# Norms of a two-block network in two parts of the tokens, 384-token matmul ranges, and weight splits two tiles ahead

## The reference

```python
x = x + mix @ w_out                                  # out-projection
h2 = rmsnorm(x, norm2_w)                             # y = x * rsqrt(mean(x*x) + eps) * w, over a token's features
x = x + jnp.square(jax.nn.relu(h2 @ w_ff1)) @ w_ff2  # MLP, 4096 wide
```

## Time and profile before

| | us |
|---|---|
| median of 3 runs | 2395.6 |
| all runs | 2392.7, 2411.45, 2395.6 |
| profiled execution, its own time | 2409.31 |
| its span in the profile | 2407.5 |
| PE busy in the span | 2305.8 |
| mean granted PE clock, of full speed | 0.983 |

### The profile page before, as it was taken

One profiled execution on the slowest core, in us unless ns is written; L12 is line 12 of the kernel. 1 busy time (PEld: TensorE's weight loads), 2 busy tenths in 40 slices (PEclk: granted clock), 3 DMA queues, 4 the chain that ended last, 5 costly groups with the idle time before them and its releaser, 6 DMA issues.

```text
span 2407.5 us, 29863 instructions
## 1 busy us (share of the span) xinstructions
PE 2305.8 (96%) x11514; PEld 1828.8 (76%) x11514; DVE 1409.9 (59%) x2253; ACT 901.5 (37%) x1536; POOL 514.6 (21%) x385
## 2 busy tenths in 40 slices
PE   7989799999999998989999999999999999999998
PEld 5655577888877875668888888888776568888887
DVE  5475648888667456773565565543635774534435
ACT  4254533232333224882422222122422684423232
POOL 2332214232312210001312121111120001322221
PEclk9999899999999999999999999999999999999999
DMA  4211016555411221011243343321122112222321
GB/s 162 88 62 54 27 35 235 193 192 203 167 66 57 93 96 34 22 36 36 84 140 123 118 136 123 123 101 59 58 96 80 32 45 70 102 89 96 109 88 53
DMA packets 76248, 227.69 MB, mean 95 GB/s; under 512 B 9151, under 2 KB 12608, under 8 KB 76108
## 3 DMA queue, kind: packets, MB, share of 16 engines
q1 hardware_dynamic: 70928, 216.69, 26.5%
q0 software_dynamic: 1856, 6.07, 0.7%
q10 hardware_dynamic: 3324, 3.02, 0.4%
HBM read 220.99 MB, written 4.76 MB: 94 GB/s over the span
## 4 chain that ended last, share of the span: by engine, by line
PE 84%; DVE 7%; ACT 4%; issue 3%; POOL 2%; ACTq 0%; DMA 0%; DVEq 0%; SPq 0%; POOLq 0%
PE psum L685 33%; PE psum L949 25%; PE psum L1256 3%; PE psum L715 3%; PE psum L654 3%; PE psum L1287 2%; PE psum L735 2%; PE psum L1210 2%; PE psum L1145 1%; PE psum L1271 1%; PE psum L603 1%; PE psum L1104 1%; PE psum L1223 1%; PE psum L1171 1%; DVE mod_scratch L1440 1%
## 5 line engine op out<-in xcount | busy, mean ns | idle before, releaser
L685 PE MATMUL psum<-mix_split,weight_split 128*128 128x512 f32 (+1 forms) x3456 | 701.3, 364 | 2.3 <-POOL weight_split L2743 1.3
L685 PEld LDWEIGHTS psum<-mix_split,weight_split 128*128 128x128 f32 x3456 | 589.8, 188 | 110.4 <-POOL weight_split L2743 1.7
L949 PE MATMUL psum<-hidden,weight_split 128*128 128x512 f32 (+1 forms) x3072 | 623.2, 364 | 0.6 <-DVE residual L1736 0.6
L949 PEld LDWEIGHTS psum<-hidden,weight_split 128*128 128x128 f32 x3072 | 523.5, 188 | 96.9 <-DVE weight_split L1362 1.0
L2193 ACT CAST weight_split<-weight_ring 128x1024 fp32r<-128x1024 f32 x269 | 277.1, 1041 | 298.4 <-PE psum L949 235.6
L2743 POOL TENSOR_TENSOR weight_split<-weight_ring,weight_split 128x1024 fp32r<-128x1024 f32 x89 | 233.0, 2618 | 597.1 <-ACT weight_split L2193 596.5
L1721 DVE TENSOR_TENSOR hidden<-hidden_tmp,hidden 128x512 fp32r<-128x512 f32 (+1 forms) x128 | 156.0, 1238 | 305.9 <-POOL hidden_tmp L2864 305.9
L1362 DVE TENSOR_TENSOR weight_split<-weight_ring,weight_split 128x1024 fp32r<-128x1024 f32 x180 | 233.8, 1301 | 39.8 <-ACT weight_split L2193 39.8
L2864 POOL TENSOR_TENSOR hidden_tmp<-hidden_tmp 128x512 f32<-128x512 f32 (+1 forms) x128 | 127.5, 1007 | 598.3 <-ACT hidden L2446 598.0
L2442 ACT ACTIVATE hidden_tmp<-psum 128x512 f32<-128x512 f32 (+1 forms) x128 | 69.2, 541 | 482.8 <-PE psum L685 481.8
L1738 DVE SCALAR_TENSOR_TENSOR residual<-psum,modulation,residual 128x512 f32<-128x512 f32 x192 | 120.2, 657 | 156.3 <-PE psum L949 155.9
(11 more groups left out here) (317 smaller groups left out, 2483.7 us busy)
## 6 DMA issues: line engine op xcount, KB each, us to landing
weight_ring<-in_w_mlp SPq DMA_DIRECT2D x128, 512.0 KB, 3.8
weight_ring<-in_w_ff SPq DMA_DIRECT2D x64, 512.0 KB, 4.4
mod_ring<-in_w_mod SPq DMA_DIRECT2D x48, 512.0 KB, 3.5
late_ring<-in_w_mod SPq DMA_DIRECT2D x96, 256.0 KB, 3.4
weight_ring<-in_w_in SPq DMA_DIRECT2D x45, 512.0 KB, 3.5
weight_ring<-in_w_out SPq DMA_DIRECT2D x24, 512.0 KB, 3.4
weight_ring<-in_tables SPq DMA_DIRECT2D x13, 512.0 KB, 3.5
weight_ring<-in_w_v SPq DMA_DIRECT2D x8, 512.0 KB, 3.9
```

The costliest lines, as they stand in the source:

```text
L685: m = pe.matmul(psum[:, b + r, 0:hi - lo], w[:, part_w, :], x[:, part_x, k, lo:hi], start=k == 0 and part_w + part_x == 0, stop=k == KT - ...
L949: mm = pe.matmul(psum[:, b + r, 0:hi - lo], w[:, part_w, :], G[:, part_x, f % (2 * GROUP), lo:hi], start=jj == 0 and part_w + part_x == 0, ...
```

## The change

It has four pieces.

1. **384-token ranges.** Copy 0's out-projection (tiles 0 to 3), up products (from tile 2 on) and down products (all groups but the last) take `halves_of(0) = [(0, 384), (384, 768)]` in place of 512 and 256. ACT's relu and square then cover both banks in one instruction, and DVE adds the result to `X` in three pieces (0:384, 384:512, 512:768), since the gate differs from token 512 on.
2. **Norms in two parts.** For `n2` and `l1n2` the parts are tokens 0 to 255 and 256 to 511; for `l0n2` and `l1n1` tokens 0 to 511 and the context. The last four output tiles ahead of the norm (all eight down tiles for `l1n1`) are made for the first part and then for the second, with the first part's sums and spread between the second part's tiles, and no `keep_busy`. The next product's first two tiles follow in the same two parts, with the second part's sums and spread between their input tiles.
3. **Splits two weight tiles ahead** in the in-projection (`in2_two_on`) and out-projection (`two_on`), whatever tables lie between.
4. **The first two tiles of `w_out2`** are now declared before the mid stage's tables, and split at the end of the in-projection; the split in the attention is gone.

The diff, cut to its core (ACT and POOL follow DVE's order):

```diff
+        def parts_of(norm):
+
+            cut = S if norm in ("l0n2", "l1n1") else S // 2
+            return [(norm + "a", 0, cut), (norm + "b", cut, T2 if cut == S else S)]
...
+        def up_spans(ranges, f):
+
+            return XB if len(ranges) > 1 and f < 2 else [(0, ranges[-1][1])]
...
+        def halves_of(l):
+
+            return X1 if l else [(0, T2 // 2), (T2 // 2, T2)]
...
+        def two_on(name, m):
+
+            return load_at[name(m + AHEAD)] if m + AHEAD < KT else load_at[name(m)] + AHEAD
+
+        def in2_two_on(l, i):
+
+            return load_at["w_in2", (l, IN2[i + AHEAD][0])] if i + AHEAD < 14 else load_at["w_in2", (l, IN2[i][0])] + AHEAD
...
+            def part_sums(norm, p):
+
+                tag, lo, hi = parts_of(norm)[p]
+                token_sums(tag, [sums_and_last(tag, SQ[:, 0, :], SQ[:, 1, :], lo, hi)], (tag + "_act", ("root", lo)), 0)
+
+            def part_spread(norm, p):
+
+                tag, lo, hi = parts_of(norm)[p]
+                b = on_all_partitions(tag, (hi - lo) // P, c=lo, n=1)
+                freed[b] = [(tag + "_vec", ("scaled", KT - 1, 0))]
+
             def norm(tag, nt, last, squares=None):
 
...
+            def product_in_parts(tag, tiles, x, spans, order=range(KT)):
+
+                at = [use_load(*w, split=True) for _, w in tiles]
+                for p, (lo, hi) in enumerate(spans):
+                    for (i, _), load in zip(tiles, at):
+                        j = split_at[load]
+                        b = bank_of[tag, i, p] = take()
+                        if p == 0:
+                            pe.wait_ge(*when(lo_of(j), j))
+                        wait_bank(b)
+                        for k in range(KT):
+                            w = WS[:, j % SPLIT_RING, :, order[k] * P:(order[k] + 1) * P]
+                            for part_w, part_x in ((0, 0), (0, 1), (1, 0)):
+                                m = pe.matmul(psum[:, b, 0:hi - lo], w[:, part_w, :], x[:, part_x, k, lo:hi],
+                                              start=k == 0 and part_w + part_x == 0, stop=k == KT - 1 and part_w == 1)
+                        m.then_inc(*did("gemm", (tag, i, p)))
+                        freed[b] = [(tag + "_vec", ("add", i, ("part", p)))]
+                        split_use[j] = (tag, i, p)
+                        yield i, p
+
+            def out_and_norm(tag, tiles, x, norm, order=range(KT)):
+
+                for i, p in product_in_parts(tag, tiles, x, [part[1:] for part in parts_of(norm)], order):
+                    if (i, p) == (4, 1):
+                        part_sums(norm, 0)
+                    if (i, p) == (5, 1):
+                        part_spread(norm, 0)
+
+            def pair_in_parts(tag, tiles, x, norm, evac, sums_at, spread_at):
+
+                bs = []
+                for i, _ in tiles:
+                    bs.append(take(2))
+                    bank_of[tag, i] = bs[-1]
+                at = [use_load(*w, split=True) for _, w in tiles]
+                for p, (part, lo, hi) in enumerate(parts_of(norm)):
+                    place = (0, 0) if p == 0 else (1, 0) if lo == S else (0, lo)
+                    steps = product_as_made(tag, tiles, x, [(lo, hi)], lambda k: part_ready(part, k), evac, bs, at, places=[place], ends=p == 1)
+                    for step, _ in enumerate(steps):
+                        if (p, step) == (0, sums_at):
+                            part_sums(norm, 1)
+                        if (p, step) == (0, spread_at):
+                            part_spread(norm, 1)
...
+                            else:
+                                product(tag + "_up", [(f, w1(f)) for f in fs], HS, ranges, None, up_evac)
+                    if g == NGROUP and next_norm:
+                        down_in_parts(tag, w2, G, next_norm)
+                    elif g > 0:
...
+            def down_in_parts(tag, w2, G, norm):
+
...
 
             def block_1():
                 pools["row"], pools["gla"], pools["turn"], pools["gemm"] = [0, 1], [2, 7], [4, 5], [6, 7]
                 mixers()
...
-                x_ready = lambda k: ((norm_tag + "_act", ("hi", k, 1)), (norm_tag + ("_pool" if k % 2 else "_vec"), ("lo", k, 1)))
-                product(tag, [(i, ("w_in2", (l, IN2[i][0]))) for i in range(2)], HS_2, in2_span(l, 0), x_ready, evac)
+                pair = [(i, ("w_in2", (l, IN2[i][0]))) for i in range(2)]
+                if l == 0:
+                    x_ready = lambda k: ((norm_tag + "_act", ("hi", k, 1)), (norm_tag + ("_pool" if k % 2 else "_vec"), ("lo", k, 1)))
+                    product(tag, pair, HS_2, in2_span(l, 0), x_ready, evac)
+                else:
+                    bs = [take(2) for _ in pair]
+                    for (i, _), b in zip(pair, bs):
+                        bank_of[tag, i] = b
+                    at = [use_load(*w, split=True) for _, w in pair]
+                    steps = product_as_made(tag, pair, HS_2, X1, lambda k: part_ready(norm_tag + "a", k), evac, bs, at)
+                    for step, _ in enumerate(steps):
+                        if step == 3:
+                            part_sums(norm_tag, 1)
+                        if step == 6:
+                            part_spread(norm_tag, 1)
                 for i in range(2, 14):
+                    if l and i == 4:
+                        for k in range(KT - 2, KT):
+                            for name, key in part_ready(norm_tag + "b", k):
+                                pe.wait_ge(*when(name, key))
                     product(tag, [(i, ("w_in2", (l, IN2[i][0])))], HS_2, in2_span(l, i), None, evac)
                     next(filt, None)
...
                 next_split[l] = len(split_use)
+                for m in range(2):
+                    use_load("w_out2", (l, m), split=True)
                 hi_all = streams[-1][1]
...
-                    yield from product_as_made(out, tiles, HS_T2, RG, lambda i: ((f"mix2_{l}_act", ("hi", i)), mix2_lo(l, i)),
-                                               lambda m, r: (out + "_vec", ("add", m, r)), bs, at, MIX2)
+                    at = [load_at[w] for _, w in tiles]
+                    yield from product_as_made(out, tiles, HS_T2, halves_of(l), lambda i: ((f"mix2_{l}_act", ("hi", i)), mix2_lo(l, i)),
+                                               lambda m, r: (out + "_vec", ("add", m, last_piece(halves_of(l), r))), bs, at, MIX2)
 
                 making = [iter(())]
                 for _ in make_pair(0):
...
+                add_part(5, 1)
+                split_lo(last + 2)
+                for t, _ in enumerate(normed_part(norm, 0, HS, gain, shift)):
+                    if t == 1:
+                        add_part(6, 1)
+                    if t == 3:
+                        add_part(7, 1)
+                inverse_part(norm, 1)
+                split_lo(last + 3)
+                for _ in normed_part(norm, 1, HS, gain, shift):
+                    pass
+
+            def out_tiles(tag, name, ranges, norm_tag, gate):
+                for ms in [(0, 1)] + [(i,) for i in range(2, PARTED)]:
                     for m in ms:
-                        stage(*name(m))
+                        split_lo(two_on(name, m))
                     for m in ms:
-                        for r, (a, z) in enumerate(ranges):
-                            if r == 0:
+                        for p, (r, a, z, c) in enumerate(pieces_of(ranges)):
+                            if p == 0:
                                 ve.wait_ge(*when("gemm", (tag, m)))
-                            x, ps = X[:, m, a:z], psum[:, bank_of[tag, m] + r, 0:z - a]
+                            x, ps = X[:, m, a:z], psum[:, bank_of[tag, m] + r, c:c + z - a]
                             if gate is None:
...
                 for i in range(2, 14):
-                    stage("w_in2", (l, IN2[i][0]))
+                    split_lo(in2_two_on(l, i))
                     evac(i)
...
                     h, k0 = units[u][0], units[u][3]
                     first = k0 == 0 and i == 0
-                    if first and h == MH - 1:
-                        split_lo(load_at["w_out2", (l, 0)] + 1)
                     if first and h % 2 == 0:
                         for _ in making[0]:
...
                 sy.dma_start(ST[u % 4][:, :], strip).then_inc(strip_sem[u % 4], 16)
             fill(load_at["w_ff1", 2])
-            sy.wait_ge(*when("n2_vec", ("scaled", KT - 1, 0)))
+            sy.wait_ge(*when("n2b_vec", ("scaled", KT - 1, 0)))
             for v in range(2):
...
             fill(places[0] + AHEAD)
-            sy.wait_ge(*when("l0n2_vec", ("lo", KT - 2, 1)))
-            sy.wait_ge(*when("l0n2_pool", ("lo", KT - 1, 1)))
+            sy.wait_ge(*when("l0n2b_vec", ("lo", KT - 2, 0)))
+            sy.wait_ge(*when("l0n2b_pool", ("lo", KT - 1, 0)))
```

396 lines of the change are left out of this document (293 added, 103 removed).

## The result

Over 20 executions of each on one chip the changed kernel takes 2389.6 us (median; 2384.4 to 2392.5), the kernel before 2408.4 (2392.7 to 2413.7): ratio 0.9925, 95% interval [0.9913, 0.9937], a gain of some 18 us. The forecast was 2360, range 2346 to 2384: too low, and the range missed it too. The change is faster, but by less than the 1% that "faster" was to mean. The profiled execution of the changed kernel took 2386.9 us, 22.4 less than the profiled execution of the kernel before, where the sum of the terms was 35.

The account below looks back on a forecast made before the run. PE, at 96% of the span, was taken as the bound. Ranges 9.0, attention 6.3, splits 6.0, half clock 5 and norms 8.8 sum to 35 us, off the median 2395.6: forecast 2360, range 2346 to 2384.

Parts of the forecast that it names:

- Ranges, 9.0: Copy 0's MLP: 1392 pairs of 384-column matmuls gain 0.0065 us each at the quick pace, 9.0 us; ends 0 and 15.
- a gain in PE's work holds for both: Sum step: 35 us comes off the profiled 2409.3 and equally off the shown runs' median 2395.6, 13.7 below it.
- Attention, 6.3: Last head of each attention: PE's waits of 3.70 and 2.59 us go once w_out2's splits leave, 6.3 us.
- Two tiles ahead, 6.0: In-projection: split waits of 2.54, 1.06, 1.77 (copy 1) and 1.02 (copy 0) go, 0.4 left, 6.0 us.
- all end with a cast that could have stood earlier: In-projection: reason given for counting all four split waits, 6.4 us, as removable.
- Half clock, 5: 1.4 us lost behind waits at five places, three in copy 1's in-projection, two in last heads; 5 us, ends 0 and 7.
- n2 and l1n2, 0: Two norms split at token 256: gain about 1, at n2 waited out again behind SP's late load; 0, ends -4 and +2.
- l0n2, 3.4: Norm l0n2 in two parts: 8.5 + 1.3 gained, less 4.4 sums and spread and 2 waits, 3.4 us.
- l1n1, 5.4: Norm l1n1 in two parts: 8.5, 2.4 from the in-projection pair, 0.9 from down products, less 4.4 and 2, 5.4 us.
- DVE behind POOL's split: Warning: DVE low parts lose up to 2 us behind POOL's weight split at three norms; sum some 30, not 35.
- ranges free: Rival, 0.20: two 384-column matmuls take what 512 and 256 take; 26 us remain, 2370 us.
- the norms give nothing: Rival, 0.13: second part's chain late at every norm, clock falls in waits; norms and clock give 0, 2374 us.

Follow-up runs that it names:

- e9: Changed kernel with norm l1n1 whole again, as in the kernel before; 2386.0 us, ratio 0.9931 to the kernel before.
- e11: Kernel before with in-projection splits two weight tiles ahead and copy 1's filter column sums one tile later; 2393.1 us, ratio 0.9960.
- e3b: Kernel before with only the in-projection's weight splits moved to two weight tiles ahead; 2404.1 us, ratio 0.9982.
- e15: Changed kernel with 16 small matmuls in the wait before copy 1's filter column sums; 2381.5 us, ratio 0.9895 to the kernel before.
- e10: Changed kernel with 34 small matmuls in the wait before copy 1's filter column sums; 2388.1 us, ratio 0.9947 to the kernel before.
- e6: Changed kernel with the load of n2's fourth up tile issued ahead of SP's wait; 2380.9 us, ratio 0.9904 to the kernel before.
- e13: Kernel before, unchanged, profiled once more; its profiled execution took 2409.8 us.
- e16: Changed kernel with l1n1 whole, copy 1's column sums a tile later and the fourth up tile's load early; 2371.5 us, ratio 0.9846 to the kernel before.
- e8: Changed kernel with copy 1's column sums a tile later and the fourth up tile's load early; 2377.4 us, ratio 0.9895 to the kernel before.
- e5: Changed kernel with copy 1's filter column sums and their reciprocal one weight tile later; 2378.4 us, ratio 0.9895 to the kernel before.

## Where the forecast held and where it failed

- **Ranges, 9.0**: 483.51 in the kernel before to 474.67 in e9, which has the changed ranges and the whole norm, is 8.8; 50.88 to 49.92 in the up products ahead of it 1.0 more. Right, with a condition that I had missed: it is the gain over an execution at the slow pace. Over a quick one it is 0 (474.55 in e11, with 512 and 256). The Trainium skill's rule that the prediction names (TensorE: Matmul & The Clock Gate, section Back-to-back issue gap: a fixed 2.5 ns for each matmul, so ranges worth 0) misses the slow pace but gives the right answer against the quick one.
- **The level: the step "a gain in PE's work holds for both" failed.** The 9 us of the ranges are taken from the profiled execution at the slow pace; in the median of three, two of them near 2394, they were probably there already. The 13.7 were no free offset. The sum against the profiled execution's own time would have been 2374, 13 short of what the changed kernel's profiled execution took; taking it off the median of three made it 26. The median of 20 executions of the kernel before is 2408.4, close to the profiled one.
- **Attention, 6.3** and two half clocks of 1.4: 4.2 + 4.2 = 8.4 us. Right, and in copy 1 in spite of the 1.37 that l1n1's new wait takes there (5.9 gained in e9, without it). No table came late.
- **Two tiles ahead, 6.0: failed.** The step "all end with a cast that could have stood earlier" is true of three of the four, and says nothing of what is late next. 2.54 was POOL's split of tile 2, which this edit doesn't move. 1.06 and 1.77 lay inside the filter chain of 19.3 us; without them the chain's end showed (0.79 to 4.45 in e3b). Only copy 0's 1.02 came in. This is the step that failed: a wait was priced as gained without asking whether a chain beside it takes just as long.
- **Half clock, 5**: wrong in both its parts. In copy 0's in-projection, for which nothing was priced, 2.9 came beside the wait of 1.02 (e3b), behind a wait that no edit touches; in copy 1 new waits of 2 to 4 us brought it back, and behind 4 us it costs 3, not 1.4 (e15 and e10).
- **n2 and l1n2, 0**: +0.7 and +0.2 in this pair of traces. SP's wait was right to the tenth: the fourth up tile starts at 370.65, forecast 370.6, and e6 shows what it withheld, 3.9. But what stands behind that wait was left out: 120 matmuls take 28.9 us at first at half clock, 27.2 at e6's pace. The +0.7 hides this, since in the kernel before an earlier half clock reaches into the out-projection. Where it hardly does (e13 and e3b), it is 85.4 and 85.2 us from the third out tile to the first down product, in the changed kernel 87.1: the change costs 1.7 or a little more at n2.
- **l0n2, 3.4**: 3.2 for its stretch, less the 1.0 of the ranges in it: 2.3. Right to about 1 us.
- **l1n1, 5.4: failed.** Its start gave 5.4 (e9) with the down products. The 2.4 from a quicker pair didn't come: the pair and the wait behind it take 16.1 us, as before (15.8), though that wait fell from 2.54 to 0.60. PE waits in the pair for the second part's squares and reciprocal (0.57, 0.15 and 0.52), and on DVE the first part's tiles alternate with the second part's additions. And the second part stands in ACT's and DVE's queues ahead of the pair's evacuation, which the forecast did not look at, and 1.37 us are lost at the end of attention 1. Undone, the end comes 4.4 us (e9) or 2.7 (e16 against e8) sooner.
- **DVE behind POOL's split**: the row of 2.48 at 1703.14 began 0.9 us after POOL's split (1702.25 to 1704.64) and ended at 1705.62, 0.3 behind POOL's next low part, where its kind takes 0.48. At l1n2 the same instruction takes 2.27 beside POOL's split of 2014.69. That is some 2 us of DVE at two of the norms, and the warning was in place, though at l1n2 PE loses nothing by it (+0.2).

The rivals: ranges free is refuted against this profile; "the norms give nothing" was nearest, since l1n1 took back what l0n2 gave, and its 2374 by the median fails by the same offset. Its 21 us off the profiled execution would be 2388, near the 2386.9 measured, but partly by luck: it counts the 6.0 of the splits, and leaves out the clock's gain in copy 0 and in the attentions.

What stays open is what picks the pace of a 512/256 pair. At n3 a second variation is plainer: between its sums and the pair the traces differ by 3 us (14.8 to 18.1) with equal waits, at a granted clock of 0.83 (the changed kernel, 704 to 724 us) or 1.00 (e5). The Trainium skill (TensorE: Matmul & The Clock Gate, section What's actually happening) says that where the clock changes varies between runs of one kernel; these traces agree, and so 3 us in one trace's stretch is not an effect. Open too is how much of the pieces' sum is owed to that: single traces of equal code differ by 3 to 4 us ahead of attention 0.

## What to carry to other kernels

Before a wait is priced as gained, follow the chain that runs beside it to its next meeting point with the engine: if that chain's length is the same with and without the wait, the wait is its cover and is worth nothing. When a norm is cut so that its second half runs beside the next product, list what that half is queued ahead of on each engine, the evacuation of that product first. And before a sum is taken off another execution than the profiled one, find out what makes the executions differ: it may be the very thing the change removes.

## What the runs showed of the hardware

- One program has two paces of its alternating 512- and 256-column matmuls, 0.3533 and 0.3467 us a pair at granted clock 1.00, each kept over a stretch of 475 to 484 us; two of 384 columns take 0.3467.
- After 4.0 us without work the granted clock is 0.50 and costs 3 us in the changed kernel (1.6 in e9, 3.7 in e3b, after 4.4 us); 3.5 us of small matmuls in that wait keep it at 1.00 and win that back (e15).
- A DVE instruction of 0.48 us takes 2.48 and 2.27 beside POOL's weight splits of 2.39 and 2.41 us (changed kernel, 1703.14 and 2015.11).
- A 128x32 matmul of 128 float32 columns issues as two records of 109 ns, 0.218 us.
- Between executions of equal code the clock at n3 is 0.83 or 1.00, 3 us apart.
